# Tokens fetched tile by tile and a first norm taken on token rows, in a two-layer decoder step

## The reference

```python
def _rms_norm(x, g):
    y = x * lax.rsqrt(jnp.mean(x * x, axis=-1, keepdims=True) + RMS_EPS)
    return y * g
...
for i in range(DEPTH):
    h = _rms_norm(x, ln_g[i]); z = h @ w_in[i]      # 1024 -> 9776 columns
    ba, ca, xa, za, q, kc, vc, ks, vs, kw, vw, g_br, zb, g_mix = split(z)
    ya = ba * conv3(ca * xa)                        # short causal convolution
    yb = sparse_attention(q, ...)                   # compressed, selected and window branch
    x = x + (sig(g_a) * (silu(za) * ya) @ W_a + sig(g_b) * (silu(zb) * yb) @ W_b) @ W_o
    x = x + sigmoid(x @ W_pg) * (p[i] @ W_ple)
y = _rms_norm(x, final_g)
```

## Time and profile before

| | |
|---|---|
| median of 3 runs | 2470.28 us (2467.87 to 2471.29) |
| profiled execution | 2474.38 us, span 2472.6 us |
| TensorE busy | 2369.0 us, 96% of the span |
| VectorE, ScalarE, GpSimd busy | 1233.0, 990.4, 208.4 us |
| read from and written to memory | 249 and 44 MB |

### The profile page before, as it was taken

How to read it: one execution, slowest core, us unless ns; L and a number is a source line. 1 busy time by engine, 2 the same in 40 slices (tenths; PEclk the granted TensorE clock), 3 DMA queues, 4 the chain that set the end, 5 groups by cost and what they waited for, 6 DMA issues and landing times.

```text
span 2472.6 us, 45716 instructions
## 1 busy us (share of the span) xinstructions
PE 2369.0 (96%) x18043; PEld 2069.5 (84%) x18043; DVE 1233.0 (50%) x2325; ACT 990.4 (40%) x2029; POOL 208.4 (8%) x349
## 2 busy tenths in 40 slices
PE   5999999999999999989989999999999999998998
PEld 4999999998788755579979999999977885555998
DVE  4444222455675566654454432224557655665543
ACT  4222222525564455532332221234446444554332
POOL 0000000000000123320000000000000002334000
PEclk9999999999999999999989999999999999999998
DMA  5333254535743467773233433546086318867530
GB/s 181 120 136 120 94 161 133 104 96 128 98 64 40 75 113 115 139 202 104 94 122 120 147 110 86 171 118 160 3 172 86 53 17 131 126 104 164 161 112 37
DMA packets 293099, 279.10 MB, mean 113 GB/s; under 512 B 92520, under 2 KB 281256, under 8 KB 291478
## 3 DMA queue, kind: packets, MB, share of 16 engines
q1 hardware_dynamic: 288470, 239.33, 44.4%
q0 software_dynamic: 4416, 36.85, 4.0%
HBM read 249.24 MB, written 43.53 MB: 118 GB/s over the span
## 4 chain that ended last, share of the span: by engine, by line
PE 80%; SPq 6%; DVE 6%; ACT 3%; DMA 2%; issue 2%; DVEq 1%; POOL 0%; ACTq 0%
PE ps L749 46%; PE ps L939 9%; PE ps L865 7%; PE ps L1064 2%; PE ps L1088 2%; PE ps L1049 2%; SPq L538 2%; PE ps L1186 2%; DVE chL L1985 2%; PE ps L892 1%; PE ps L964 1%; SPq L548 1%; SPq L522 1%; ACT chH L1551 1%; DMA w_raw<-in_w_out_b 1%
## 5 line engine op out<-in xcount | busy, mean ns | idle before, releaser
L749 PE MATMUL ps<-hH,wH 128*128 128x272 f32 x2048 | 427.0, 290 | 16.8 <-DVE hL L1837 16.7
L749 PE MATMUL ps<-hH,wL 128*128 128x272 f32 x2048 | 428.0, 290 | 0.0
L749 PE MATMUL ps<-hL,wH 128*128 128x272 f32 x2048 | 424.9, 289 | 0.0
L408 DVE TENSOR_TENSOR wL<-w_raw,wH 128x2048 fp32r<-128x2048 f32 (+1 forms) x108 | 248.4, 2300 | 344.3 <-ACT wH L399 342.2
L749 PEld LDWEIGHTS ps<-hH,wH 128*128 128x128 f32 x2048 | 324.4, 189 | 20.1 <-issue 16.3
L749 PEld LDWEIGHTS ps<-hH,wL 128*128 128x128 f32 x2048 | 323.3, 190 | 0.0
L749 PEld LDWEIGHTS ps<-hL,wH 128*128 128x128 f32 x2048 | 323.2, 189 | 0.0
L1985 DVE TENSOR_TENSOR chL<-ps,chH 64x256 fp32r<-64x256 f32 x512 | 216.5, 423 | 159.0 <-ACT chH L1551 151.3
L1551 ACT ACTIVATE chH<-ps 64x256 fp32r<-64x256 f32 x512 | 206.8, 404 | 215.4 <-PE ps L939 206.8
L399 ACT ACTIVATE wH<-w_raw 128x2048 fp32r<-128x2048 f32 (+1 forms) x108 | 206.6, 1913 | 98.6 <-PE ps L749 77.6
L719 POOL TENSOR_SCALAR pr<-pr,inv,zg 128x512 f32<-128x512 f32 (+3 forms) x256 | 153.0, 607 | 973.0 <-DVE inv L2177 973.0
(11 more groups left out here) (318 smaller groups left out, 4010.2 us busy)
## 6 DMA issues: line engine op xcount, KB each, us to landing
w_raw<-in_w_in SPq DMA_DIRECT2D x60, 1024.0 KB
craw<-in_cache_kv SPq DMA_DIRECT2D x256, 128.0 KB, 5.1
w_raw<-in_w_in SPq DMA_DIRECT2D x64, 256.0 KB
k_sel<-in_cache_kv SPq DMA_DIRECT2D x128, 128.0 KB, 5.5
v_sel<-in_cache_kv SPq DMA_DIRECT2D x128, 128.0 KB, 10.2
out_new_win_sample<-in_state_win POOLq DMA_DIRECT2D x16, 1016.0 KB, 5.7
w_raw<-in_w_out_a SPq DMA_DIRECT2D x8, 1024.0 KB
k_win<-in_state_win SPq DMA_DIRECT2D x16, 512.0 KB, 7.0
```

Source lines behind the costliest of these rows:

```text
L408: dve.tensor_tensor(block_part(wL, b), block_part(w_raw, b), block_part(wH, b).bitcast(F32), ALU.subtract).then_inc(w_lo, 1)
L749: last = nc.tensor.matmul(ps[:, bank + hf, 0:HALF], st, x[:, k, hf * HALF:(hf + 1) * HALF], start=k == 0 and w is wH and x is xH, stop=k = ...
```

## The change

The first stage is written anew. SP first loads the identity matrix and epsilon (129 columns of the constants), the sample tokens and the gain of layer 0 as one row, then the prompt in four tiles of 128 tokens, each with a semaphore of its own, then the weights of blocks 0 (in two halves of 4 chunks) and 1; the other constants and the state rows come behind them. The norm is taken on rows, tokens on partitions: ScalarE squares a tile with a running sum per row and takes the root of one value per token, VectorE takes the reciprocal and scales the row (`xs`). TensorE turns the scaled rows, chunk by chunk, for `hH` and `hL`, which ScalarE and VectorE make directly from PSUM with the gain `g0` as a factor per partition; and it turns the raw rows, tile by tile, for the residual `xT`. The two tiles of block 0 are made together, chunk by chunk, in four PSUM banks, with the turning of the chunk three ahead between them. The barrier is gone; the state rows are turned in block 1. The sums of the other norms, the layers and the tail are as before, but for how semaphores are numbered.

```diff
             for tt in range(NT):
+                sp.dma_start(xin[:, tt, :], a["x_prompt"][0, tt * P:(tt + 1) * P, :]).then_inc(x_in[tt], 16)
+            w_first = a["w_in"][0:1].rearrange("l (k p) c -> p (l k) c", p=P)
+            for k in range(0, KT, 4):
+                sp.dma_start(w_raw[:, 0, k:k + 4, 0:BW], w_first[:, k:k + 4, C_CA:C_CA + BW]).then_inc(w_in_sem[0] if k else w_half, 64 if k else 16)
+            sp.dma_start(w_raw[:, 1, :, 0:BW], w_first[:, :, C_XA:C_XA + BW]).then_inc(w_in_sem[1], 64)
...
+            rows_turned(NT, 4)
             for c in range(KT):
...
+                last = nc.tensor.transpose(ps[:, 7, c:c + 1], g_row[0:1, c * P:(c + 1) * P], ident[0:1, 0:1])
+            last.then_inc(start_pe, 1)
+            rows_turned(0, 0)
+            rows_turned(1, 2)
+            pe.wait_ge(start_dve, by_dve("scaled 4"))
             for c in range(KT):
...
+                last = nc.tensor.transpose(ps[:, 6, c * NSAM:(c + 1) * NSAM], xs[0:NSAM, NT, c * P:(c + 1) * P], ident[0:NSAM, 0:NSAM])
+            last.then_inc(start_pe, 1)
+            for c in range(3):
+                scaled_chunk(c)
+            for c in range(KT):
+                first_chunk(c)
+                if c + 3 < KT:
+                    scaled_chunk(c + 3)
+                elif c == 5:
+                    rows_turned(2, 4)
+                elif c == 7:
+                    rows_turned(3, 6)
...
+            for tt in (NT, 0, 1, 2, 3):
+                rows = P if tt < NT else NSAM
+                act.wait_ge(x_in[tt], 16 if tt < NT else 48)
+                act.activation(squares[0:rows, :], xin[0:rows, tt, :], ACT.Square, accum_out=rs0[0:rows, tt:tt + 1])
+                act.drain()
+                act.activation(rs0[0:rows, tt:tt + 1], rs0[0:rows, tt:tt + 1], ACT.Sqrt, bias=C("eps", rows), scale=1.0 / D).then_inc(start_act, 1)
+                if tt == 2:
+                    act.wait_ge(start_dve, by_dve("sample"))
+                    act.activation(hH[:, :, SEQ:TOK], hs_f[:], ACT.Copy).then_inc(start_act, 1)
+            first_high(0)
+            for c in range(KT):
+                act.wait_ge(start_pe, by_pe("chunk %d" % c))
+                act.activation(hH[:, c, 0:SEQ], ps[:, 4 + c % 4, :], ACT.Copy, scale=g0[:, c:c + 1]).then_inc(h_hi, 1)
+                if c == 1:
+                    first_high(4)
+                elif c == 4:
+                    make_high(act, 0, 1)
+            residual_rows(2, 4)
+            residual_rows(3, 6)
...
+            scaled_rows(0)
+            scaled_rows(1)
+            dve.wait_ge(start_pe, by_pe("scaled sample"))
+            dve.tensor_tensor(hs_f[:], ps[:, 6, 0:KT * NSAM].rearrange("p (c t) -> p c t", t=NSAM), g0[:].unsqueeze(2).to_broadcast([P, KT, NSAM]),
+                              ALU.mult).then_inc(start_dve, 1)
+            residual_rows(0, 0)
+            scaled_rows(2)
+            residual_rows(1, 2)
+            scaled_rows(3)
```

More of the change, by code:

```diff
@@ L84 @@
 CONST, NCONST = _const_layout()
+CFIRST = P + 1
 def constants():
@@ L474, in step_before_last, with by_pe, by_act, by_dve @@
             return nth(c_mm, 4 * (10 * l + (5 if n == 6 else n)) + j - 1)
+        FROM_PE = ["rows 4", "gain", "rows 0", "rows 1", "scaled sample"] + ["chunk %d" % c for c in range(KT)] + ["rows 2", "rows 3", "columns"]
+        FROM_ACT = ["root 4", "root 0", "root 1", "root 2", "high sample", "root 3", "high weights", "rows 2", "rows 3", "masks"]
+        FROM_DVE = ["scaled 4", "rows 4", "gain", "scaled 0", "scaled 1", "sample", "rows 0", "scaled 2", "rows 1", "scaled 3",
+                    "low sample", "low weights", "columns"]
+        def by_pe(step):
+            return FROM_PE.index(step) + 1
+        def by_act(step):
+            return FROM_ACT.index(step) + 1
+        def by_dve(step):
+            return FROM_DVE.index(step) + 1
         block = ctx.enter_context(nc.Block())
@@ new lines, in scaled_chunk, with first_chunk @@
+            def scaled_chunk(c):
+                if c >= 4:
+                    pe.wait_ge(h_lo, c - 3)
+                elif c == 0:
+                    pe.wait_ge(start_dve, by_dve("scaled 3"))
+                for tt in range(NT):
+                    last = nc.tensor.transpose(ps[:, 4 + c % 4, tt * P:(tt + 1) * P], xs[:, tt, c * P:(c + 1) * P], ident)
+                last.then_inc(start_pe, 1)
+            def first_chunk(c):
+                if c == 0:
+                    pe.wait_ge(start_dve, by_dve("low weights"))
+                elif c == 4:
+                    w_ready(0, 0)
+                pe.wait_ge(h_lo, c + 1)
+                for jj in range(2):
+                    for w, x in ((wH, hH), (wH, hL), (wL, hH)):
+                        for hf in range(2):
+                            last = nc.tensor.matmul(ps[:, 2 * jj + hf, 0:HALF], w[:, 0, c, jj * P:(jj + 1) * P], x[:, c, hf * HALF:(hf + 1) * HALF],
+                                                    start=c == 0 and w is wH and x is hH, stop=c == KT - 1 and w is wL)
+                    if c == KT - 1:
+                        last.then_inc(tile, 1)
@@ L1451, in _ @@
+            for l in range(NL):
+                if l:
+                    norm_std(l, rstd)
+                    for c in range(KT):
+                        act.wait_ge(h_f, KT * (l - 1) + (c + 1))
+                        act.activation(hH[:, c, :], t_f[:, c % 2, :], ACT.Copy).then_inc(h_hi, 1)
                 for i in range(4):
@@ L1829, in _, with first_low, scaled_rows @@
-            end_phase(dve)
-            make_low(dve, 0, 0)
+            def first_low(k):
+                if k:
+                    dve.wait_ge(w_hi, 1)
+                else:
+                    dve.wait_ge(start_act, by_act("high weights"))
+                dve.tensor_tensor(wL[:, 0, k:k + 4, 0:BW], w_raw[:, 0, k:k + 4, 0:BW], wH[:, 0, k:k + 4, 0:BW].bitcast(F32), ALU.subtract
+                                  ).then_inc(w_lo if k else start_dve, 1)
+            def scaled_rows(tt):
+                rows = P if tt < NT else NSAM
+                dve.wait_ge(start_act, by_act("root %d" % tt))
+                dve.reciprocal(rs0[0:rows, tt:tt + 1], rs0[0:rows, tt:tt + 1])
+                dve.drain()
+                dve.tensor_scalar(xs[0:rows, tt, :], xin[0:rows, tt, :], rs0[0:rows, tt:tt + 1], None, ALU.mult).then_inc(start_dve, 1)
@@ new lines, in _ @@
+            scaled_rows(3)
+            dve.wait_ge(start_act, by_act("high sample"))
+            dve.tensor_tensor(hL[:, :, SEQ:TOK], hs_f[:], hH[:, :, SEQ:TOK].bitcast(F32), ALU.subtract).then_inc(start_dve, 1)
+            first_low(0)
+            for c in range(KT):
+                dve.wait_ge(h_hi, c + 1)
+                dve.scalar_tensor_tensor(out=hL[:, c, 0:SEQ], in0=ps[:, 4 + c % 4, :], scalar=g0[:, c:c + 1], in1=hH[:, c, 0:SEQ].bitcast(F32),
+                                         op0=ALU.mult, op1=ALU.subtract).then_inc(h_lo, 1)
+                if c == 1:
+                    first_low(4)
+                elif c == 4:
+                    make_low(dve, 0, 1)
```

213 lines of the change are left out of this document (119 added, 94 removed).

## The result

The changed kernel takes 2440.2 us in the median (2439.8 to 2441.2, 4 runs), the kernel before 2470.8 us beside it (2467.9 to 2472.5, 4 runs). The ratio is 0.9878, with a 95% interval of 0.9861 to 0.9895: 30.6 us less, where 20.6 were forecast with a range to 25.3. The direction was right and the range was missed on its far side. This is the first comparison; later ones are new executions with the kernel before beside them. The profiled execution took 2440.02 us, its span 2438.2 us.

A forecast was written before the change was run, and what follows sets the result against it. TensorE, busy 96%, was taken as the bound, so an earlier block 0 is kept. 18.0 + 18.3 + 1.0 + 0.8 = 38.1 against 58.7 gives 20.6 us less, 2449.7 us; range 2446 to 2454, with rivals 2445 to 2462.

The forecast's parts named there:

- The first matmul at 18.0: Start of block 0: tokens, transposes, then VectorE's copies and scalings let the first matmul start at 18.0, against 42.95 before.
- The loop takes 4.5 + 16.3 x (1 - 4.5 / 28.8) = 18.3: Block 0's chunk loop: 18.3 us, with the clock rising 4.5 us after the first matmul; bounds 16.3 and 18.9.
- the 6.0 of the earlier trace: Kernel before, first layer matmuls: the clock rose 6.0 us after the first matmul, used as the late bound.
- 54 x 0.1258 = 6.8, so block 0 ends at 58.7 now: Kernel before, from 51.94 us: 54 matmuls remain in block 0, taking 6.8 us, so it ends at 58.7.
- Ten hand-overs at 0.1 us more than I have counted: 1.0: Waits between engines on the new start's path: 1.0 us added to the end of block 0.
- State rows 0.8: Nine small transposes of state rows, moved onto the path in block 1: 0.8 us added.
- the transfers that it meets are issued behind work of the same engines, so they move with it: Chain behind block 0: later transfers shift along with the engines, so the early start's gain is kept.
- The clock did not stay low in the loop: Rival: clock stays low through block 0's loop, 28.8 us instead of 18.3; gain 8.6, 2461.7 us; chance 16%.
- No piece was late: Rival: first loads, tile 3 or first weights, land 6 us later; gain 14.6, 2455.7 us; chance 10%.
- No change: Rival: early start given back at a later transfer that does not move with the engines; 2470 us; chance 4%.
- slower: Rival: the missed clock stays at 1.2 GHz in block 1 and behind, 5 us lost after 27 us; chance 4%.

The follow-up runs named there:

- first held execution: Changed kernel with its first load held back by 18 idle VectorE additions (24.7 us), first comparison: 2470.4 us, ratio 1.0008 against the kernel before.
- the second: The same kernel held by 18 additions, profiled again in a later comparison beside the unheld changed kernel: 2469.5 us, ratio 1.0001 against the kernel before.
- six held executions: Profiled executions of the changed kernel with its start held back by idle VectorE additions; holds of 3 to 30 additions took 2447.7 to 2484.6 us in the mean.

## Why the prediction was off, point by point

**The first matmul at 18.0: right,** in part by errors that cancel. It came at 17.80. Tile 0 landed at 5.73 (5.5), the path went over VectorE's copies and scalings from 10.48 (10.3) to 14.96, 4.5 us for 4.9 and 0.3 of hand-overs, then 12 transposes in 2.82 (2.4).

**"The loop takes 4.5 + 16.3 x (1 - 4.5 / 28.8) = 18.3": the formula held, the term in it was too large.** The clock rose 2.9 us after the first matmul; with that the formula gives 17.6, and the loop took from 17.80 to 35.39, 17.6. The choice lay too near the 6.0 of the earlier trace rows; over the five profiled executions the rise came at once to 3.1 us after it.

**"54 x 0.1258 = 6.8, so block 0 ends at 58.7 now": one chunk too few.** At 51.94 the seventh chunk of tile 0 begins, so 60 matmuls are still to do. Block 0 ended at 59.8, 1.1 us later, and the gain is larger by as much.

**"Ten hand-overs at 0.1 us more than I have counted: 1.0": they cost nothing.** There is no idle TensorE in the loop; VectorE and ScalarE have slack in each chunk, as the prediction itself said, so hand-overs there could not show.

**State rows 0.8:** 0.70.

These make the start 3.1 us better than the forecast, 23.7 by its sum and 23.5 at the second `cv_u`, and 24.1 in the mean of five executions, where the clock rose earlier. With the start right the forecast would have been 2470.3 - 24.1 = 2446.2, still inside the range, near its edge.

**What failed beyond that is the step "the transfers that it meets are issued behind work of the same engines, so they move with it".** It let the rest cost the same wherever it begins. Of the 27.3 us by which the means of all executions differ, 24.1 are the start and 3.2 ± 1.4 lie behind it. They are made of low clock, late transfers and the pause of TensorE, which the old and the new kernel did not meet alike. The first comparison showed 3.3 us more still: the median of its four executions of the changed kernel lay 2.3 below the mean of 22 and that of before 1.0 above the mean of 114. That is within the spread of single executions and is put down to chance here; the range had nothing in it for either, only bounds of the start. So of the 10.0 us between forecast and measurement, 3.5 are the start, 3.2 the rest and 3.3 the draw of the first executions.

**The rivals.** The clock did not stay low in the loop. The Trainium skill's rule (TensorE: Matmul & The Clock Gate, Part 4: PE-mode transpose), that work in transpose mode does not bring the full clock, is spoken against below. No piece was late: the loads kept the forecast times. No change and slower did not happen; the long run of matmuls stayed unbroken.

**What is open:** why the rest costs 2 to 3 us more at some moments, and what of the 3.2 us is the moment and what the code. The stretches of low clock, the late window transfer and the pause are seen in the rows; what sets them off was not isolated.

## What to carry to other kernels

Read the gain of a new start at one mark that both versions have, in several profiled executions, and hold the new version back by that time: if the old time comes back, the start is the change and the code adds nothing in sum. Then compare place by place too, for an equal sum can be made of different pieces. And a long piece of DMA in the chain is not its cost; that is what the engine behind it waited. Behind a moved start, don't count on the rest to the microsecond: give the range 2 to 4 us for it, and as much again for medians of four executions. And two tiles made chunk by chunk cover the making of the next weights, which one tile alone does not: that was worth 4 us of the start here, half of them clock that was not lost.

## What was not expected of the hardware

**The clock rose with nothing but transposes.** In the first held execution TensorE had been idle since the start of the span, then did 16 small transposes and these (timeline):

```profile
30.53 3.68 PE L783 MATMUL ps<-con,xin 128*128 128x128 f32 x16 [0.36 <-DMA xin<-in_x_prompt]
34.14 0.68 PE L820 MATMUL ps<-con,xs 32*128 32x32 f32 x8
```

while the same eight took longer in the second:

```profile
34.00 1.06 PE L820 MATMUL ps<-con,xs 32*128 32x32 f32 x8
```

With the loads reordered alone, the weight loads of the same five transposes quickened at their end:

```profile
17.47 0.96 PEld L761 LDWEIGHTS ps<-con,xin 32*128 32x128 f32 x5 [0.33 <-issue]
18.75 0.60 PEld L761 LDWEIGHTS ps<-con,xin 32*128 32x128 f32 x5 [0.33 <-issue]
```

No matmul of another kind had run in either. So float32 transposes alone brought the pace of 2.4 GHz here, in seven of the twenty profiled executions and not in the others; the first stage of before, with 10.35 us of them, had not shown it. The Trainium skill (TensorE: Matmul & The Clock Gate, Part 4: PE-mode transpose) has it that work in transpose mode does not bring the full clock, and these rows differ from it; that they ran in that mode no row says, since the trace names them MATMUL.

**A clock gained early can be lost again.** In the first held execution TensorE stood idle for 4.58 us while VectorE copied and scaled, and its granted clock fell; over this window it is 0.54 in the mean:

```profile
37.00:44.00 7.00, 4.60 (x20) 4.28 (x21) 6.17 (x9) 3.98 (x6) 0.00 (x0) 0.54 0.95 331
```

The pace of 2.4 GHz was back 2.0 us after the first matmul of block 0 at 42.17. In all six held executions in which the transposes had quickened, the granted clock was down at 0.50 before block 0 began, so the early clock gained nothing.
